# Mixture-of-experts stage of a one-core encoder block: blocks of 32 slots in four column groups, gathered by one-hot products in every block, with three expert buffers

## What is computed

```
h = rmsnorm(x, g_ffn)
lg = h @ w_rg + b_rg                    # 8 groups, the best one is taken
le = h @ w_re + b_re                    # 8 experts in that group, the best two are taken
out[token] += weight * ((silu(h @ w_g[e]) * (h @ w_u[e])) @ w_d[e])    # for both experts e
```

## Time and profile before

| | us |
|---|---|
| median of three runs | 1318.48 |
| span of the profiled execution | 1317.8 |
| dense stage (to the first expert load behind it) | 359.1 |
| routing, until the first product with expert weights | 359.1 to 383.8 |
| positions that gather | 383.8 to about 640 |
| positions that don't | about 640 to 1289.8 |
| from the last product to the end | 28.0 |

### The profile page before, as it was taken

One profiled execution on the slowest core, in us unless ns is written; L12 is line 12 of the kernel. 1 busy time (PEld: TensorE's weight loads), 2 busy tenths in 40 slices (PEclk: granted clock), 3 DMA queues, 4 the chain that ended last, 5 costly groups with the idle time before them and its releaser, 6 DMA issues.

```text
span 1317.8 us, 15984 instructions
## 1 busy us (share of the span) xinstructions
PE 1145.9 (87%) x5149; PEld 559.4 (42%) x5150; DVE 364.1 (28%) x720; ACT 234.4 (18%) x496; POOL 227.7 (17%) x271
## 2 busy tenths in 40 slices
PE   6999999999999999999888898877788777887881
PEld 5788776778853333333322222222222222222220
DVE  3899334354355222222210101001000010000005
ACT  4232324573110000000010111001100011000012
POOL 3455444083000000010001011000010000100010
PEclk9999999999999999999999999999999999999996
DMA  6431211234069999999999889999999999999684
GB/s 227 125 126 64 97 70 61 98 122 192 19 261 377 362 412 419 418 414 423 384 427 425 352 365 428 432 430 429 427 431 430 429 428 430 427 423 422 283 379 194
DMA packets 56837, 417.15 MB, mean 317 GB/s; under 512 B 10384, under 2 KB 10541, under 8 KB 26090
## 3 DMA queue, kind: packets, MB, share of 16 engines
q1 hardware_dynamic: 51354, 411.45, 75.4%
q0 software_dynamic: 5312, 5.28, 1.2%
q10 hardware_dynamic: 144, 0.07, 0.0%
HBM read 410.45 MB, written 18.36 MB: 325 GB/s over the span
## 4 chain that ended last, share of the span: by engine, by line
PE 45%; DMA 42%; DVE 6%; ACT 3%; issue 2%; SPq 1%; POOL 0%; DVEq 0%; POOLq 0%; ACTq 0%
DMA sb_weights<-in_w_exp_up 40%; PE ps_proj L1775 13%; PE ps_proj L1492 10%; PE ps_scores L1795 6%; PE ps_proj L1722 4%; PE ps_proj L1543 2%; DVE ps_scores L1015 1%; PE ps_proj L1670 1%; PE ps_proj L1674 1%; PE ps_proj L1667 1%; PE ps_proj L1622 1%; PE ps_proj L1625 1%; PE ps_proj L1628 1%; PE ps_aT L1784 1%; DMA sb_weights<-in_w_exp_gate 1%
## 5 line engine op out<-in xcount | busy, mean ns | idle before, releaser
L1775 PE MATMUL ps_proj<-sb_weights,sb_scratch 128*64 128x512 f32 x1984 | 461.1, 616 | 52.1 <-DMA sb_weights<-in_w_exp_up 49.7
L1775 PEld LDWEIGHTS ps_proj<-sb_weights,sb_scratch 128*64 128x64 f32 x1984 | 159.9, 141 | 344.3 <-issue 341.7
L1795 PE MATMUL ps_scores<-sb_weights,sb_scratch 128*64 128x512 f32 x992 | 228.5, 597 | 21.8 <-ACT sb_scratch L938 21.8
L1376 DVE TENSOR_TENSOR sb_scratch<-sb_scratch,ps_proj 128x256 f32<-128x256 f32 x62 | 26.1, 421 | 549.0 <-ACT sb_scratch L936 549.0
L695 POOL TENSOR_TENSOR sb_tick<-sb_tick 1x1 f32<-1x1 f32 x62 | 11.5, 185 | 851.5 <-ACT sb_scratch L943 851.5
L1795 PEld LDWEIGHTS ps_scores<-sb_weights,sb_scratch 128*64 128x64 f32 x992 | 67.0, 136 | 145.6 <-issue 109.5
L1492 PE MATMUL ps_proj<-sb_hT_r,sb_ring_r 128*128 128x512 f32 x512 | 123.9, 394 | 0.0
L936 ACT ACTIVATE sb_scratch<-ps_proj 128x256 f32<-128x256 f32 x62 | 23.8, 384 | 495.9 <-PE ps_proj L1775 495.9
L1492 PEld LDWEIGHTS ps_proj<-sb_hT_r,sb_ring_r 128*128 128x128 f32 x512 | 94.8, 188 | 26.7 <-issue 6.5
L640 POOL TENSOR_TENSOR sb_ring_r<-sb_ring,sb_ring_r 128x1024 fp32r<-128x1024 f32 x32 | 76.2, 2392 | 65.0 <-ACT sb_ring_r L755 64.0
L943 ACT ACTIVATE sb_scratch<-ps_scores 128x512 f32 (+1 forms) x62 | 37.0, 597 | 269.1 <-PE ps_scores L1795 269.1
(11 more groups left out here) (314 smaller groups left out, 879.6 us busy)
## 6 DMA issues: line engine op xcount, KB each, us to landing
sb_weights<-in_w_exp_up SPq DMA_DIRECT2D x59, 2048.0 KB, 14.7
sb_weights<-in_w_exp_down SPq DMA_DIRECT2D x59, 2048.0 KB, 10.4
sb_weights<-in_w_exp_gate SPq DMA_DIRECT2D x59, 2048.0 KB, 22.1
sb_ring<-in_w_in SPq DMA_DIRECT2D x9, 2048.0 KB, 8.7
sb_x<-in_x SPq DMA_DIRECT2D x8, 512.0 KB, 5.1
sb_dense<-expert_rows SPq DMA_DIRECT2D x4, 1024.0 KB, 8.1
sb_ring<-in_w_conv_pw SPq DMA_DIRECT2D x1, 2048.0 KB, 9.0
sb_ring<-in_w_attn_up SPq DMA_DIRECT2D x1, 2048.0 KB, 7.7
```

What stands on the lines that cost most here:

```text
L1376: dve.tensor_tensor(act, gsig, ps_gu[:, 256:512], ALU.mult).then_inc(act_ready, 1)
L1775: last = mm(ps_gu[g * BLK:(g + 1) * BLK, :].rearrange("p (a n) -> p a n", a=2), hTb[:, c, half * BLK:(half + 1) * BLK], weights[:, slice(6 ...
L1795: last = mm(ps_y[g * BLK:(g + 1) * BLK, :], actT[:, j, half * BLK:(half + 1) * BLK], weights[:, place(parity, 4 + half), 2 * j + g, :], st ...
```

## The change

- Blocks have 32 slots. Every product of the experts and the gather works in four column groups of 32 with 256 columns: gate and up 32 matmuls, down 16, gather 16. The activations need one transpose, the gathered rows two.
- Every position gathers its rows with one-hot products, one position ahead. The array `hTs` and its copies are gone. ACT makes the copies of rows that DVE made.
- `weights` holds three experts. A position belongs to class (position mod 3), an expert to class (order mod 3), where order counts down from expert 63 in a numbering across the groups. Each expert is loaded once. Three experts are fixed at the start (63, 55, 47), and the first five in order (also 39 and 31) get at least one block even if they have no rows. All classes run for the same number of rounds; the experts behind the first of a class that is shorter start later by the difference.
- The load for position p waits for gate and up products of position p - 3.
- SP issues six thirds behind the dense stage's last product and not four. The down third of the third expert lies where the routing's temporaries are and is issued after `slots_done`, behind the gate and up thirds of the fourth load.

The core of the diff:

```diff
-BLK = 64
-AHEAD = 2
+BLK = 32
+NG = P // BLK
+NBUF = 3
+FIRST = 5
...
+    put("turn", np.where(pos[None] % NBUF == cls, pos[None] // NBUF, -1))
+    put("always", order < FIRST)
+    put("movable", order >= NBUF)
...
-            for i in range(3):
-                load_third(0, i, zero, in_w)
-            load_third(1, 0, one, in_w1)
+            load_first(0, 0)
+            load_first(1, 1)
+            load_first(1, 2)
+            load_first(1, 0)
+            load_first(2, 1)
+            sp.wait_ge(logits_done, 1)
+            load_first(2, 0)
 
             sp.wait_ge(listed, 1)
...
+            def load_gate_up(n, e, base, free):
+                sp.wait_ge(in_w[0], 16 * n)
+                sp.wait_ge(gu_done, free)
+                sp.sem_inc(place_free, 1)
+                load_third(base, 0, e)
+                sp.wait_ge(in_w[1], 16 * n)
+                load_third(base, 1, e)
...
+            values = load_values(NBUF)
+            load_gate_up(NBUF, *values)
+            sp.wait_ge(slots_done, 1)
+            load_first(2, 2)
+            load_down(NBUF, *values)
+            n_loads = sp.value_load(loads_i, min_val=FIRST, max_val=NE)
+            with sp.Fori(NBUF + 1, n_loads) as n:
+                values = load_values(n)
+                load_gate_up(n, *values)
+                load_down(n, *values)
...
+                link(dve.tensor_tensor(eblk, eblk, const("always", NE), ALU.max))
+                link(dve.tensor_scalar(used, eblk, 1.0, None, ALU.min))
...
+                link(dve.tensor_scalar(own_turns, own_turns, -1.0, rounds, ALU.mult, ALU.add))
+                link(dve.tensor_scalar(turn_lo, own_turns, const("movable", NE), ps_tables[0:NE, 8:9], ALU.mult, ALU.add))
...
+                link(dve.tensor_scalar(free_after, first_pos, float(1 - NBUF), None, ALU.add))
...
+            static_onehot(0)
+            count_blocks()
+            static_onehot(1)
+            static_onehot(2)
+            place_turns()
             gate_and_up(0)
+            list_loads()
+            take_loads()
+            place_rows()
+            gate_and_up(1)
+            next_onehot(0, 0)
             prepare_slots()
...
+            def gather(p, c):
+
+                pe.wait_ge(hot_b, p + 1)
+                for t in range(T):
+                    for g in range(NG):
+                        last = mm(ps_rows[g * BLK:(g + 1) * BLK, 0:QCOLS], onehots[c][:, t, :],
+                                  h2[:, t, g * QCOLS:(g + 1) * QCOLS], start=t == 0, stop=t == T - 1)
+                last.then_inc(rows_done, 1)
...
+                for r in range(KD):
+                    rows = hTb[:, r % 2 * P + r // 2 * BLK:r % 2 * P + (r // 2 + 1) * BLK]
+                    at = 6 * c + r // 4
+                    for g in range(NG):
+                        cols = slice(g // 2 * 256 + g % 2, g // 2 * 256 + 256, 2)
+                        last = mm(ps_gu[g * BLK:(g + 1) * BLK, 0:2 * P].rearrange("p (a n) -> p a n", a=2),
+                                  rows, weights[:, at:at + 3:2, r % 4, cols], start=r == 0, stop=r == KD - 1)
...
+            gate_up(1, 1, 2)
+            gather(2, 2)
+            transpose_act(1)
+            transpose_rows(2)
+            slot_rows()
+            down(1, 1, 2)
+            gate_up(2, 2, 3)
...
+            with pe.Fori(1, n_rounds) as r:
+                for c in range(NBUF):
+                    p = NBUF * r + c
+                    loads = pe.value_load(loads_at[0:1, bass.ds(p, 1)], min_val=1, max_val=NE)
+                    gate_up(p, c, loads)
+                    gather(p + 1, (c + 1) % NBUF)
+                    transpose_act(p)
+                    transpose_rows(p + 1)
+                    down(p, c, loads)
```

More of the change, by code:

```diff
@@ L76 @@
 for _n, _w in [("ident", P), ("before", P), ("ones", P), ("pos", BLK), ("block", MAXPOS),
[L77 to L79 removed]
+               ("flip", P), ("lane8", EPG), ("row", 2 * T), ("quarter", 1), ("mask", P),
+               ("turn", MAXPOS), ("class_before", NE), ("class_of", NBUF), ("class", 1), ("base", 1), ("expert", 1),
+               ("always", 1), ("movable", 1), ("bucket", 5 * P)]:
     CONST[_n] = (_at, _w)
@@ new lines, in block_kernel @@
+        gbest, code, m1, m2, d_e, gden, eden = (late_temp(T) for _ in range(7))
+        ecount, eblk, used, unused, first_pos = (late_temp(1, rows=NE) for _ in range(5))
+        turn_lo, turn_hi, rounds, own_turns, load_no, load_next, free_after = (late_temp(1, rows=NE) for _ in range(7))
+        own_hot, ecmp = late_temp(NBUF, rows=NE), late_temp(SEQ // BLK, rows=NE)
+        first_of, rank_of, steps_of, pos_of, slot_of = (late_temp(2 * T) for _ in range(5))
+        steps = late_temp(2 * T, SEQ // BLK)
@@ L954, in _ @@
+            copy_rows(0)
+            rows_to_block(0)
+            for c in range(NBUF):
+                position(c, c, 0)
+            act_e.wait_ge(listed, 1)
+            n_rounds = act_e.value_load(rounds_i, min_val=2, max_val=ROUNDS)
+            with act_e.Fori(1, n_rounds) as r:
+                for c in range(NBUF):
+                    position(NBUF * r + c, c, r)
             for t in range(T):
@@ L1415, in _ @@
[L1415 removed]
+            for c in range(NBUF):
+                list_rows(c, c, 0)
             weigh_choices()
[L1418 to L1423 removed]
@@ L1436, in _ @@
+            with dve.Fori(1, n_rounds) as r:
+                for c in range(NBUF):
+                    p = NBUF * r + c
+                    gate_and_up(p)
+                    next_onehot((c + 2) % NBUF, p - 1)
+                    list_rows(p, c, r)
             yb = dense[:, 0:T * 2048].rearrange("p (t k d) -> p t k d", t=T, k=2)
@@ new lines, in transpose_act, with down @@
+            def transpose_act(p):
+                pe.wait_ge(act_ready, p + 1)
+                pe.transpose(ps_actT[:, 0:P], act, ident).then_inc(actT_done, 1)
+            def down(p, c, loads):
+                pe.wait_ge(actT_ready, p + 1)
+                pe.wait_ge(in_w[2], 16 * loads)
+                for k in range(NG):
+                    for g in range(NG):
+                        last = mm(ps_y[g * BLK:(g + 1) * BLK, 0:QCOLS], actT[:, k * BLK:(k + 1) * BLK],
+                                  weights[:, 6 * c + 4 + k // 2, k % 2 * 2 + g // 2, g % 2 * QCOLS:(g % 2 + 1) * QCOLS],
+                                  start=k == 0, stop=k == NG - 1)
+                last.then_inc(down_done, 1)
@@ L1727, in transpose_rows @@
-            def transpose_rows():
-                for c in range(4):
-                    last = pe.transpose(ps_hTb[:, c * P:(c + 1) * P], rows_sb[:, c * P:(c + 1) * P], ident)
-                last.then_inc(hTb_done, 1)
-            pe.wait_ge(hot_b, 1)
-            gather()
-            pe.wait_ge(rows_ready, 1)
-            transpose_rows()
-            def rest_of_experts():
-                pe.wait_ge(rest_ready, 1)
-                mm(ps_oT[:, 0:NE], erest_b, before[0:NE, 0:NE], start=True, stop=True).then_inc(rest_done, 1)
@@ new lines, in _ @@
+            transpose_rows(0)
+            turns_of_classes()
+            gate_up(0, 0, 1)
+            first_row()
+            gather(1, 1)
+            transpose_act(0)
+            transpose_rows(1)
+            load_rows()
+            down(0, 0, 1)
+            gate_up(1, 1, 2)
[5 more added lines that the diff above has]
+            gate_up(2, 2, 3)
+            gather(3, 0)
+            transpose_act(2)
```

737 lines of the change are left out of this document (258 added, 479 removed).

## The result

| | before | after |
|---|---|---|
| median of the runs, us | 1319.12 | 1336.41 |
| lowest to highest of 4 runs | 1318.29 to 1320.92 | 1334.88 to 1338.32 |
| span of the profiled execution | 1317.8 | 1336.5 |

The ratio is 1.0125, with a 95% interval of 1.011 to 1.0141. The change makes the kernel 1.25% slower. The forecast was 1325.0, 0.5% slower: the direction and the range held, the size didn't.

A forecast was written before the change was run, and what follows sets the result against it. PE slightly bounds the gathering positions, loads the long second part. Queue from 427.0 plus 2.6, 837.1 for 168 thirds and 20.1 of gaps, last position 9.7, end 28.0 less 0.2: span 1324.3, median 1325.0; range 1313 to 1346.

The forecast's parts named there:

- last position: Behind the last load's up third: a position's 8.0 us of PE plus 1.7 for the low clock, ending at 1296.5.
- end: From PE's last product to the kernel's end: 28.0 us before, less 0.2 for the shorter copy.
- Load pace: Distance of two gate issues in the long second part, taken from the kernel before: 14.95 us a load, 4.98 a third.
- the pace as a rival: Rival "faster": loads come closer than 14.95 us, each 0.1 less worth 6.0; with 14.7 it is 1310; chance 0.14.
- Start: Behind the dense stage: queue restarts at 407.6, gaps of 18.6 us ahead of gate 3 and 4.5 ahead of down 3.
- Number of loads: Expert loads over the whole kernel: 60 and not 59, since expert 31 is loaded without rows; + 15.0 us of transfers.
- Position on PE: PE's products for one position: 8.0 us against 12.5 before, if four column groups overlap as two do; hidden under loads.
- Three-block experts: Experts 61, 59, 60 at positions 22, 26, 27: loads for 31 and 34 lose 10.9 and 9.2 us, sum 20.1.
- What costs nothing: ACT's copies, about 1.7 us a position, and POOL's 72 scatters at 0.99 are hidden by the loads, 7 us of cover.
- Clock: PE falls to 1.2 GHz at most positions, hidden under loads; costs 1.7 us each where loads wait for PE after idling.
- the rival that feeds the groups too slowly: Rival on PE's column groups: at 70 ns a pair a position takes 10 us, the kernel 1345; chance 0.08.

## Why the prediction was right in direction and short in size

The forecast span was 1324.3, the measured one 1336.5. What the prediction said of the mechanism held: the loads set the time, one load more costs its full price, PE is hidden behind the loads except at the gaps. Two terms of its sum were too small. The price of a load was put at 14.95 us and measured 15.05. The start was priced as if position 2's down products ran at the full clock, and the queue was called full from 427.0 us on; its end came 5.4 us late. The 12.2 us divide by the steps of the prediction as follows.

| step | forecast | measured | us |
|---|---|---|---|
| start, to the up third of the eighth load | 489.3 | 494.7 | + 5.4 |
| load pace, 52 loads from there | 14.95 | 15.055 | + 5.4 |
| gaps at three-block experts | 20.1 | 21.8 | + 1.7 |
| last position | 9.7 | 9.9 | + 0.2 |
| end | 27.8 | 27.3 | - 0.5 |

(489.3 is 1286.8 less 52 loads and 20.1; 494.7 is the issue at 474.91 and the 19.75 us that lie between the last gate issue, 1279.51, and the start of its products. 52 loads and the gaps took 804.6 us, and less 66.9 for three of them that is 15.055 for each of the other 49.)

- *Load pace: the term that failed most.* It was taken over from before, and is worth 5.4 us in the 52 loads and 0.4 in the part of the start that runs at it. Why it is 0.1 us more with the change is open: the written rows cost less than before, and the 0.18 us that remain without them were not found. I named the pace as a rival only with a smaller value, and held the share of 1.01 for a floor. It isn't one: the share is 1.01 at 426 and at 428 GB/s, and at intervals from 14.65 to 15.05. A value carried over to a changed kernel needs a bound on both sides like any other.
- *Start.* Gate 3 was issued at 408.3 (forecast 407.6), which is close for a chain of so many terms. Then two things were missed. The sentence on the clock has 1.7 us for each place "where the loads wait for PE behind such an idle time", but the start doesn't apply it: position 2's down waited 15.66 us and then took 3.64 and not 1.93. Down 3, which waits for it, was issued at 430.2 (the second of the two at 409.32) and not at 427.0: 0.7 from gate 3, 0.5 since the three thirds took 18.0 us to use and not 17.5, and 2.0 from the down products and the hand-over. And "from here the queue is full" was wrong at the next load but one: gate 5 waits for gate and up of position 5, which run from 447.25 to 451.06, and is issued at 451.36, which costs another 1.8. Part of this is the clock again, since gate and up of position 3 had taken 5.04 and not 3.82. With 0.4 from the pace this makes the 5.4. The experiment with the down third first removed both with one exchange in the order of issues.
- *Number of loads.* Right: 60, and the experiment without the load of expert 31 gave back 13.7 us in the medians for its 15.0.
- *Position on PE.* Right, 8.17 us start to start for 8.0. The assumption that four groups overlap like two was the large uncertainty of the prediction, and the row nearest to it decided well: a step of 256 columns in four groups took 0.454 us (3.63 / 8), the forecast was 0.427, so 0.94 of full overlap. The Trainium skill, page TensorE: Matmul & The Clock Gate, section Part 3, Measured speedup vs the span model, has 2.38 times for three column tiles. As an estimate carried over to four groups, 0.79 of full, it gave the prediction's 9.9 us (worked out again, 9.8); this trace, with 0.94 and 8.17, doesn't agree. No run here has three groups.
- *Three-block experts.* Right in place and size (21.8 for 20.1), and experiments with the order and with the idle rounds moved them as worked out.
- *What costs nothing.* That the gather is hidden in the long part is right: doubling it cost time only at the gaps and at the end. For the copies that went to ACT and for the scatters no run tests it; ACT is busy for 43 and POOL for 32 of the 380 us in the stretch above.
- *Clock.* Right for most positions of the long part, where it is hidden, and at the end: the last gate and up took 5.41 and not 3.82, with a granted clock of 0.50, the lower level of 1.2 GHz.

That the measured time lies in the range is in part luck: its upper end came from the rival that feeds the groups too slowly, which didn't happen, and nothing in the prediction bounded the pace from above. That shorter positions would gain nothing in the long part was right. What I left unsaid is that the idle rounds at positions 4 and 7, which I described as a help ("PE passes in 8 us each while two loads come"), were the costliest part of the change: they push the fourth load from position 4 to position 5, and set the three-block experts closer. 24 us came back when they were moved, 8.6 of them (21.8 less 13.2) at the three-block experts, the rest at the start.

## What to carry over

When loads set the time, count the moments at which their queue is dry, and for each find the one issue that waits: here one line that moved idle rounds, and one exchange in the order of issues, were worth 24 and 11 us, while 144 us less of PE (three eighths of gate and up and half of the gather left out) were worth 17. An issue that is late by SP's clock costs nothing as long as the thirds ahead of it are still under way. And a steady pace measured in one kernel is a result of that kernel, not a constant.

## What the runs showed that I had not expected

- The rate of a saturated stream of loads depends on small things beside it: 14.65, 14.78, 14.83, 14.95 and 15.05 us for the same 6.29 MB in kernels of this study, each the median of 24 or 25 intervals. Most of these lie within a few hundredths of it; single ones are 0.2 to 0.5 off. Rows written beside it cost 0.22 us a load (4.2 MB in all by the page's DMA queues, 1 KB pieces) and 0.30 (the same bytes in 2 KB pieces); 256-byte pieces cost nothing that shows; entries that write nothing cost 0.05 for 96 of 128.
- PE's work doesn't change the pace of the loads: 14.84 with a third less of the products and 15.05 with the gather doubled are the paces of the same kernels without these edits (14.83 and 15.05).
- In the changed kernel the granted clock over the long part rises with the work: 0.76 with 212 of 380 us busy, 0.86 with 264, 0.90 with 306. The kernel before had 0.96 with 302, so the busy time alone doesn't give it. The pace of the loads was the same at 0.76 and at 0.87 (14.84 and 14.83), and at 0.86 and at 0.90 (15.05).
